# Two-chunk weight transfers over a longer part of the expert stream, and one early chunk in another buffer

## The chip, the core and the metric

The kernel runs on one core of a Trainium2 chip (trn2). The metric is device time in microseconds (us) of one launch: 1072.7 us, the median of three runs (1072.42 to 1074.67). One more execution was profiled. It took 1072.61 us, of which 1070.9 us are the span from its first to its last instruction.

In the rows, PE is TensorE's matmul side and PEld its weight load, DVE is VectorE, ACT is ScalarE, POOL is GpSimd and SP is SyncE, which here does little but wait on semaphores and issue DMAs.

## The reference

One encoder layer is computed for 320 tokens (256 of a prompt, 64 of a running stream) in float32, with D = 1024: a normalized input projection, sliding-window attention and a short convolution, an output projection, and then a mixture of 32 experts of which each token takes 4. The experts are what matters here:

```python
def expert_block(args):
    xe, e = args
    gu = xe @ w_gu[e] + b_gu[e]          # w_gu[e]: 1024 x 2048
    g, u = gu[:, :D_FF], gu[:, D_FF:]
    g = jnp.minimum(g, SWIGLU_LIMIT)
    u = jnp.clip(u, -SWIGLU_LIMIT, SWIGLU_LIMIT)
    h = (u + 1) * (g * jax.nn.sigmoid(SWIGLU_ALPHA * g))
    return h @ w_down[e] + b_down[e]     # w_down[e]: 1024 x 1024
```

All weights of all 32 experts are read from HBM once: 8 MB of `w_gu` and 4 MB of `w_down` for each, 418 MB read in all with the rest.

## The kernel before

**Work.** The attention part runs first (to about 155 us). Then the experts follow in 16 pairs. In a pair the two experts share the PE array: expert 2j fills rows 0 to 63 of the output and expert 2j+1 rows 64 to 127, so two matmuls of 64 rows go side by side. The weights of an expert are cut into 12 *chunks* of 1 MB (128 partitions x 2048 floats): chunks 0 to 7 are `w_gu`, used in `gate_up` (lines 891 to 903, matmuls on lines 896 and 898), and chunks 8 to 11 are `w_down`, used in `down` (lines 905 to 917, matmuls on lines 912 and 914). `pair(j)` computes gate and up of pair j, and then down of pair j-1; between them PE turns activations and one-hot matrices and scatters the rows of an earlier pair. Each use of a chunk adds one to the semaphore `chunk_used`; the chunks with the same number of the two experts of a pair come free practically together. `IN_USE` lists all 384 chunks in the order of their use.

**Loads.** A ring of 16 slots in SBUF receives the chunks in the order of `ORDER`, in which five chunks are left out: they have buffers of their own (`EARLY_AT`, `HALVES_AT`, `GU_AT`, `PIECES_AT`, `LATE_AT`) and are loaded once, by SP, before the ring comes round. 379 chunks go through the ring; here they are numbered 0 to 378 in load order. Chunk n goes to slot (n+1) mod 16. SP issues all loads from one queue, in order. A load of chunk n waits until chunk n-16, which had the slot before, has been used, that is until `chunk_used` has reached that chunk's place in `IN_USE` (line 495). Where SP waits, every later load waits behind it.

**One or two chunks to a transfer.** Lines 361 to 367 plan the transfers. Two chunks can go in one DMA if they are neighbours in HBM (an even chunk and the next one of the same expert) and lie in neighbouring slots. In `ORDER` such two stand next to each other, whereas `IN_USE` alternates between the experts; so the stretch with single transfers at the beginning (`EARLY` entries) and at the end (`FINE` entries) is copied from `IN_USE`. A two-chunk load waits for the later of its two slots, and both chunks count as landed when all of it has. Before the change chunks 0 to 36 go singly, two-chunk transfers run from chunk 37 to chunk 343 (with three single ones in between, where the alignment breaks at the left-out chunks), and chunks 344 to 376 go singly again. The last two chunks go in halves (line 502).

**PE and the loads.** PE waits for the landing of both chunks before each step of `gate_up` or `down` (`landed`, lines 886 to 889). `EARLY_AT` is chunk 11 of expert 1, a `w_down` chunk.

Of the kernel before, what the change touches and what calls it, by code (L numbers as in the profile page):

```python
# [29 lines left out]
def hybrid_layer_kernel(nc, x_prompt, x_sample, cache_k, cache_v, state_conv, norm1_g, w_in, q_norm_g,  # L30
# [14 lines left out]
    NE = w_router.shape[2]  # L45
# [16 lines left out]
    GUC, DNC = KT, FT * D // FLAT  # L62
    CH = GUC + DNC
# [7 lines left out]
    with ctx:  # L71
# [270 lines left out]
                    ORDER += [(2 * pair + s, c + a) for c in chunks[::2] for s in range(2) for a in range(2)]  # L342
        ALL = len(IN_USE)

        EARLY, FINE = 2 * 2 * GUC + 2 * DNC, 4 * GUC + 4
        ORDER[:EARLY] = IN_USE[:EARLY]
        ORDER[ALL - FINE:] = IN_USE[ALL - FINE:]
        EARLY_AT, LATE_AT, PIECES_AT = (1, CH - 1), (NE - 2, 0), (NE - 4, 0)
        HALVES_AT, GU_AT = (1, 3), (1, GUC - 1)
        for at in (EARLY_AT, LATE_AT, PIECES_AT, HALVES_AT, GU_AT):  # L350
            ORDER.remove(at)
# [1459 lines left out]
```

How the kernel before makes its waits and increments, by code:

```python
        def most_rows(eng):  # L403
            eng.wait_ge(counts_ready, 2)
            return eng.value_load(most_i[0:1, 0:1], min_val=0, max_val=TOK)
# [25 lines left out]
        @block.sync  # L431
# [23 lines left out]
                             ).then_inc(wo_in, 16)  # L455
            sp.dma_start(w_o[:, 0:CT, :],
                         w_out[0, ATT:ATT + CONV, :].rearrange("(j p) n -> p j n", p=P)).then_inc(wo_in, 16)
            load(*ORDER[RING - 1], 1, slot_of(RING - 1))
            FIRST_DONE = RING - 2
            for n in range(RING - 2):
                slot = slot_of(n)
                if slot == FREE_SLOTS:
                    sp.wait_ge(v_done, 1)
                if slot == QKV_SLOTS:
                    for q in range(2 * FF // (4 * P)):
                        sp.dma_start(b_guT[:, :, 4 * q:4 * q + 4],
                                     b_gu[0].rearrange("e (q p a) -> q p e a", p=P, a=4)[q]).then_inc(bias_in, 16)
                    sp.wait_ge(bch_done, 3 * CT)
                if slot == BCH_SLOTS:
                    sp.wait_ge(att_mixed, NCH)
                    sp.wait_ge(conv_mixed, CT)
# [3 lines left out]
                                     rows_of(*HALVES_AT, 1)[:, n2 * D:(n2 + 1) * D]).then_inc(halves_in, 16)  # L478
                if BCH_SLOTS <= slot < BCH_SLOTS + MIX // 2 - 1:
                    sp.wait_ge(wo_used, slot - BCH_SLOTS + 1)
                if slot == BCH_SLOTS + MIX // 2 - 1:
                    sp.wait_ge(out_done, 2 * NT)
                load(*ORDER[n], 1, slot)
```

## Time and profile before

| | |
|---|---|
| median of 3 runs | 1072.7 us |
| profiled execution | 1072.61 us |
| its span | 1070.9 us |
| PE busy | 1029.8 us, 96% |
| DVE, ACT, POOL busy | 30%, 9%, 1% |
| read from HBM | 418.29 MB, 392 GB/s over the span |
| the queue of the loads (q1) | 94.7% of 16 engines' span |

The span is read in stretches: an attention part, a stretch in which the experts' work goes on without a stop, one in which PE now and then waits for a load, and an end without such waits. Busy time by stretch, the chain of waits and the DMA queue's own waits are the views used.

### The profile page before, as it was taken

Reading aid. Unit: us, or ns where it says so; the run is one execution under the profiler, and the core shown is the slowest. Engines: PE = TensorE matmul, PEld = TensorE weight load, DVE = VectorE, ACT = ScalarE, POOL = GpSimd, SP = SyncE. Lnnn points to the kernel's source line nnn. Section 1 sums busy time; section 2 is a strip of 40 time slices with the busy share of each in tenths; the row PEclk is TensorE's granted clock in tenths of the full one; section 3 lists DMA queues with packets and bytes.
Section 4 is the critical chain, followed back from the end, with each engine's and each line's share of the span. In section 5 each row is a group of like instructions: output and inputs, shape, how many; then the busy total and the mean of one; then the engine's idle time right before and its main releaser. Section 6 shows DMA issues by size and latency. Waiting matters only on the chain.

```text
span 1070.9 us, 11705 instructions
## 1 busy us (share of the span) xinstructions
PE 1029.8 (96%) x5098; PEld 491.2 (46%) x5099; DVE 317.6 (30%) x491; ACT 95.9 (9%) x165; POOL 8.3 (1%) x20
## 2 busy tenths in 40 slices
PE   8999999999999999989898989989898989999998
PEld 7767454444444444435343534434353435334333
DVE  3533031323323232312313231323223232313243
ACT  2222040100000000000001010000000000100001
POOL 1100000000000000000000000000000000000000
PEclk9999999999999999999999999999999999999999
DMA  9950969999999999999999999999999999999996
GB/s 353 317 117 1 376 232 405 419 423 424 425 420 430 427 428 428 431 427 427 430 430 427 427 430 430 427 428 428 429 428 430 427 429 429 428 415 420 422 421 256
DMA packets 57470, 420.30 MB, mean 392 GB/s; under 512 B 21061, under 2 KB 21377, under 8 KB 28257
## 3 DMA queue, kind: packets, MB, share of 16 engines
q1 hardware_dynamic: 56848, 419.32, 94.7%
q0 software_dynamic: 352, 0.55, 0.2%
q8 instruction: 20, 0.33, 0.1%
q10 hardware_dynamic: 240, 0.03, 0.0%
q14 instruction: 10, 0.07, 0.0%
HBM read 418.29 MB, written 1.58 MB: 392 GB/s over the span
## 4 chain that ended last, share of the span: by engine, by line
PE 71%; DMA 28%; SPq 0%; issue 0%; DVE 0%; ACT 0%; DVEq 0%
PE ps L896 35%; DMA ring<-in_w_gu_dram 27%; PE ps L912 7%; PE ps L820 7%; PE ps L741 5%; PE ps L938 3%; PE ps L759 3%; PE ps L617 2%; PE ps L923 1%; PE ps L898 1%; PE ps L770 1%; PE ps L942 1%; PE ps L1074 1%; PE ps L643 1%; PE ps L709 0%; DMA x<-in_x_prompt_dram 0%
## 5 line engine op out<-in xcount | busy, mean ns | idle before, releaser
L896 PE MATMUL ps<-ring,xT 128*64 128x512 f32 x1008 | 457.2, 607 | 29.0 <-DMA ring<-in_w_gu_dram 28.7
L898 PE MATMUL ps<-ring,xT 128*64 128x512 f32 x1008 | 457.7, 608 | 0.0
L896 PEld LDWEIGHTS ps<-ring,xT 128*64 128x64 f32 x1008 | 135.8, 139 | 304.4 <-issue 300.1
L912 PE MATMUL ps<-ring,he 128*64 128x512 f32 x480 | 214.2, 595 | 3.9 <-DMA ring<-in_w_down_dram 3.0
L914 PE MATMUL ps<-ring,he 128*64 128x512 f32 x472 | 211.0, 596 | 0.0
L1667 DVE TENSOR_TENSOR x<-ps,x 128x512 f32<-128x512 f32 (+1 forms) x84 | 54.3, 684 | 295.7 <-PE ps L938 268.0
L898 PEld LDWEIGHTS ps<-ring,xT 128*64 128x64 f32 x1008 | 135.9, 139 | 0.0
L912 PEld LDWEIGHTS ps<-ring,he 128*64 128x64 f32 x480 | 62.8, 137 | 133.5 <-issue 133.2
L820 PEld LDWEIGHTS ps<-oh,hn 128*128 128x128 f32 x720 | 89.5, 196 | 8.2 <-issue 6.0
L820 PE MATMUL ps<-oh,hn 128*128 128x128 f32 x720 | 91.4, 282 | 0.0
L1309 ACT COPY gu_sb<-ps 128x1024 f32<-128x1024 f32 x16 | 16.2, 1012 | 596.0 <-PE ps L898 596.0
L914 PEld LDWEIGHTS ps<-ring,he 128*64 128x64 f32 x472 | 61.8, 137 | 0.0
L1618 DVE TENSOR_TENSOR xT<-ps,g 128x512 f32<-128x512 f32 (+2 forms) x35 | 22.5, 646 | 95.9 <-PE ps L820 95.9
L1650 DVE TENSOR_TENSOR xT<-ge,xT 128x1024 f32<-128x1024 f32 x16 | 19.6, 1224 | 91.0 <-PE ps L914 91.0
L1626 DVE COPY gu_sb<-ps 128x1024 f32<-128x1024 f32 x16 | 19.6, 1224 | 90.4 <-PE ps L898 90.4
L923 PEld LDWEIGHTS ps<-ident,gu_sb 128*128 128x128 f32 x256 | 32.1, 210 | 13.0 <-issue 13.0
L938 PE MATMUL ps<-y_hi,ohT 128*128 128x512 f32 x84 | 37.8, 450 | 0.0
L1634 DVE TENSOR_TENSOR ge<-ps,b_guT 128x1024 f32<-128x1024 f32 x16 | 19.6, 1225 | 58.6 <-PE ps L923 58.6
L741 PE MATMUL ps<-xnT,w_chc 128*128 128x320 f32 x128 | 36.5, 438 | 0.0
L923 PE MATMUL ps<-ident,gu_sb 128*128 128x128 f32 x256 | 35.1, 290 | 0.0
L938 PE MATMUL ps<-y_lo,ohT 128*128 128x512 f32 x84 | 33.2, 395 | 0.0
L938 PEld LDWEIGHTS ps<-y_hi,ohT 128*128 128x128 f32 x84 | 15.7, 187 | 38.0 <-issue 36.3
(233 smaller groups left out, 633.0 us busy)
## 6 DMA issues: line engine op xcount, KB each, us to landing
ring<-in_w_gu_dram SPq DMA_DIRECT2D x102, 2048.0 KB, 25.8
ring<-in_w_down_dram SPq DMA_DIRECT2D x50, 2048.0 KB, 27.0
ring<-in_w_gu_dram SPq DMA_DIRECT2D x48, 1024.0 KB, 15.5
ring<-in_w_down_dram SPq DMA_DIRECT2D x25, 1024.0 KB, 25.3
w_chc<-in_w_in_dram SPq DMA_DIRECT2D x1, 4096.0 KB, 21.1
w_qkv<-in_w_in_dram SPq DMA_DIRECT2D x4, 768.0 KB, 9.0
w_b<-in_w_in_dram SPq DMA_DIRECT2D x1, 2048.0 KB, 28.9
w_o<-in_w_out_dram SPq DMA_DIRECT2D x2, 1024.0 KB, 28.1
```

The source lines that it names most:

```text
L617: last = mm(ps[:, QK_BANK[i], t0:t1], w_qkv[:, k, cols], xnT[:, k, t0:t1], start=(k == 0 and t0 == 0), stop=(k == KT - 1), skip_group_chec ...
L741: last = mm(ps[:, BCH_BANK[part], 0:TOK], w[:, k, col:col + P], xnT[:, k, :], start=(k == 0), stop=(k == KT - 1))
L759: last = mm(ps[0:n, OUT_BANK[t][half], :], mixed(j, t, n), w_o[:, j, half * HALF:(half + 1) * HALF], start=(j == 0), stop=(j == MIX - 1))
L820: last = mm(out[:, k % (KT // 2), 0:experts * CAP], hn[:, t, tile_features(k)], marks[:, t, 0:experts, :].rearrange("p s c -> p (s c)"), s ...
L896: even = mm(gu_banks(j)[0:CAP, n, :], xT[j % 2][:, k, 0:CAP], first[n], start=(k == 0), stop=(k == KT - 1))
L898: odd = mm(gu_banks(j)[CAP:P, n, :], xT[j % 2][:, k, CAP:P], second[n], start=(k == 0), stop=(k == KT - 1))
L912: even = mm(out[0:CAP, half, :], hid[:, f, 0:CAP], first[2 * a + half], start=(f == 0), stop=(f == FT - 1))
L914: odd = mm(out[CAP:P, half, :], hid[:, f, CAP:P], second[2 * a + half], start=(f == 0), stop=(f == FT - 1))
L923: last = nc.tensor.transpose(by_feature(banks)[:, part, f, :], gu_sb[:, features(part, f)], ident[:, :])
L938: last = mm(ps[:, half, :], ohT[:, t * P:(t + 1) * P], y[:, cols], start=(y is y_hi), stop=(y is y_lo and u not in BIASED.get(j, ())), ski ...
L1618: return V.tensor_tensor(xT[j % 2][:, tiles, :], gathered_banks(j, half)[:, first:first + n, :], g2[:, tiles].unsqueeze(2).to_broadcast([P ...
L1667: V.tensor_tensor(x[0:m, t, cols], ps[0:m, bank, :], x[0:m, t, cols], ALU.add).then_inc(added, 1)
```

## The change

Three numbers of the plan change.

```diff
-        EARLY, FINE = 2 * 2 * GUC + 2 * DNC, 4 * GUC + 4
+        EARLY, FINE = 2 * GUC + 4, 4 * DNC
         ORDER[:EARLY] = IN_USE[:EARLY]
         ORDER[ALL - FINE:] = IN_USE[ALL - FINE:]
-        EARLY_AT, LATE_AT, PIECES_AT = (1, CH - 1), (NE - 2, 0), (NE - 4, 0)
+        EARLY_AT, LATE_AT, PIECES_AT = (1, 5), (NE - 2, 0), (NE - 4, 0)
```

With GUC = 8 and DNC = 4, `EARLY` goes from 40 to 20 and `FINE` from 36 to 16. Two-chunk transfers now start at chunk 17 and end with chunk 362; 20 chunks at the beginning (17 to 36) and 18 near the end (of 344 to 362) change from single to two-chunk transfers, and the plan has 19 transfers fewer. `EARLY_AT` is now chunk 5 of expert 1, a `w_gu` chunk that pair 0 uses, so chunk 11 of expert 1 goes through the ring. Chunks 10 to 35 of the ring are thereby others than before; the number of chunks in the ring and the bytes loaded stay the same.

What a load waits for, as the count of uses in `chunk_used`, worked out from the code:

| chunks | before | after |
|---|---|---|
| 16 | 1 | 1 |
| 17, 18 | 2; 3 | 3 |
| 19, 20 | 4; 5 | 5 |
| 21, 22 | 6; 7 | 7 |
| 23, 24 | 9; 10 | 10 |
| 25, 26 | 11; 12 | 13 |
| 27, 28 | 13; 14 | 15 |
| 29, 30 | 15; 17 | 18 |
| 31, 32 | 18; 19 | 20 |
| 33, 34 | 20; 21 | 23 |
| 35, 36 | 22; 23 | 24 |
| 37 with 38 | 25 | 27 |
| 39 with 40 | 27 | 28 |
| 49 with 50 | 37 | 39 |
| 51 with 52 | 39 | 40 |
| 53 with 54 | 43 | 43 |

From chunk 53 to chunk 343 both plans are the same.

SP's instructions where the ring first comes round, before and now (`const_room` is the last piece of a left-out chunk; 128x2048 is one chunk, 128x4096 are two; - is before, + is now):

```order
 L493 DMA gatesT_room<-in_w_gu_dram 128x512
 L493 DMA const_room<-in_w_gu_dram 128x512
-L438 DMA ring<-in_w_gu_dram 128x2048 x14
-L438 DMA ring<-in_w_down_dram 128x2048 x7
+L438 DMA ring<-in_w_gu_dram 128x2048
+L438 DMA ring<-in_w_gu_dram 128x4096 x6
+L438 DMA ring<-in_w_down_dram 128x4096 x4
 L438 DMA ring<-in_w_gu_dram 128x4096 x8
 L438 DMA ring<-in_w_down_dram 128x4096 x4
```

Where 21 single loads stood, one single load and ten of two chunks stand.

SP's instructions near the end, from pair 14's loads to the last chunks:

```order
 L438 DMA ring<-in_w_gu_dram 128x4096 x2
-L438 DMA ring<-in_w_down_dram 128x4096 x2
-L438 DMA ring<-in_w_down_dram 128x2048 x4
-L438 DMA ring<-in_w_gu_dram 128x2048 x15
+L438 DMA ring<-in_w_down_dram 128x4096 x4
+L438 DMA ring<-in_w_gu_dram 128x2048
+L438 DMA ring<-in_w_gu_dram 128x4096 x7
 L438 DMA ring<-in_w_down_dram 128x2048 x14
 L502 DMA ring<-in_w_down_dram 128x2x512 x4
```

18 of 19 single loads have become nine of two chunks; the last 14 and the halves stay. On PE the number and order of matmuls are the same; only four of pair 0 now read `early_chunk`, and four of the first `down` read the ring:

```order
-L898 MATMUL ps<-ring,xT_58 64x512
-L896 MATMUL ps<-ring,xT_58 64x512
-L898 MATMUL ps<-ring,xT_58 64x512
+L898 MATMUL ps<-early_chunk,xT_58 64x512
+L896 MATMUL ps<-ring,xT_58 64x512
+L898 MATMUL ps<-early_chunk,xT_58 64x512
```

## Rows read from the trace of the kernel before

**Rows 1.** Stretches: length; busy PE, PEld, DVE, ACT, POOL; clock, DMA share, GB/s

```profile
200.00:390.00 190.00, 190.00 (x981) 86.04 (x981) 58.04 (x74) 11.30 (x11) 0.00 (x0) 1.00 1.01 425
390.00:943.00 553.00, 520.07 (x2561) 234.35 (x2559) 157.05 (x202) 31.59 (x31) 0.52 (x1) 0.98 1.01 428
943.00:977.00 34.00, 34.00 (x154) 15.34 (x156) 5.16 (x8) 0.00 (x0) 0.00 (x0) 0.95 1.00 422
977.00:1054.00 77.00, 77.00 (x359) 28.82 (x355) 28.00 (x35) 6.36 (x6) 0.00 (x0) 1.00 1.01 420
```

**Rows 2.** PE's waits from 388 to 950 us: us in total, times, longest

```profile
PE ps L896 <- DMA ring<-in_w_gu_dram: 29.0, 14, 2.7
PE ps L912 <- DMA ring<-in_w_down_dram: 3.0, 9, 0.4
```

**Rows 3.** Chain of waits, 936 to 950 us: start us, us, what

```profile
914.51 28.28 DMA ring<-in_w_gu_dram
...
942.92 0.61 PE ps L896
```

**Rows 4.** SP's waits from 186 to 213 us

```profile
SPq L438 <- PE ps L898: 25.5, 6, 5.8
```

**Rows 5.** SP's issues, narrow windows from 107.9 to 246 us: start us, us, what

```profile
107.97 0.34 SPq L438 DMA_DIRECT2D ring<-in_w_gu_dram  x1
161.29 0.33 SPq L438 DMA_DIRECT2D ring<-in_w_gu_dram  x1
190.14 0.33 SPq L438 DMA_DIRECT2D ring<-in_w_gu_dram  x1
200.18 0.81 SPq L438 DMA_DIRECT2D ring<-in_w_down_dram  x2
209.33 0.33 SPq L438 DMA_DIRECT2D ring<-in_w_down_dram  x1
212.76 0.33 SPq L438 DMA_DIRECT2D ring<-in_w_gu_dram  x1
216.20 0.33 SPq L438 DMA_DIRECT2D ring<-in_w_gu_dram  x1
245.76 0.33 SPq L438 DMA_DIRECT2D ring<-in_w_gu_dram  x1
```

**Rows 6.** DMAs issued at 107.97, 161.29 and 212.76 us: count, KB, us to landing

```profile
ring<-in_w_gu_dram SPq DMA_DIRECT2D x1, 1024.0 KB, 5.2
...
ring<-in_w_gu_dram SPq DMA_DIRECT2D x1, 1024.0 KB, 6.7
...
ring<-in_w_gu_dram SPq DMA_DIRECT2D x1, 2048.0 KB, 9.8
```

**Rows 7.** The page: DMA issues of the whole span

```profile
ring<-in_w_gu_dram SPq DMA_DIRECT2D x102, 2048.0 KB, 25.8
```

**Rows 8.** PE in order of time from 942.5 us: start us, us, what [idle before]

```profile
942.92 0.61 PE L896 MATMUL ps<-ring,xT 128*64 128x512 f32 x1 [2.12 <-DMA ring<-in_w_gu_dram]
...
943.83 1.06 PE L896 MATMUL ps<-ring,xT 128*64 128x512 f32 x1
...
947.22 0.59 PE L896 MATMUL ps<-ring,xT 128*64 128x512 f32 x1
...
947.65 0.59 PE L896 MATMUL ps<-ring,xT 128*64 128x512 f32 x1
```

**Rows 9.** DMAs issued at 995.02 and 1041.97 us: count, KB, us to landing

```profile
ring<-in_w_gu_dram SPq DMA_DIRECT2D x1, 1024.0 KB, 24.2
...
ring<-in_w_down_dram SPq DMA_DIRECT2D x1, 512.0 KB, 17.8
```

**Rows 10.** PE in order of time, its first matmuls on what these two bring

```profile
1021.58 0.57 PE ps L896
...
1060.90 0.59 PE L1089 MATMUL ps<-ring,he_last 128*64 128x512 f32 x1
```

## The prediction

> **What bounds the kernel now.** I read the busy time by stretch first. From 200 us to 1054 us the DMA engines are busy without a gap (share 1.00 to 1.01), in stretches where PE is full (190 of 190 us to 390 us, then 34 of 34 and 77 of 77 us behind 943 us) and in one where it isn't (520 of 553 us) [rows 1]. So PE works faster than the loads come, lives on the stock in the ring until about 390 us, and is held by the loads from then on: 29.0 us in 14 waits and 3.0 us in nine [rows 2]. The last of these waits ends at 942.92 us, released by a load that landed at 914.51 + 28.28 = 942.79 us [rows 3]; behind it PE has no wait for a load and sets the end. The chain that decides the time is thus: the load queue up to 942.8 us, then PE. Everything that the load queue loses before 942.8 us and that no later pause gives back is lost at the end, since the queue has no pause in which to catch up. It may seem that early loads are not critical, as PE doesn't wait for them; but an idle microsecond of the queue at 210 us is one at 943 us as well.
>
> The second question is how full the queue is. A load spends 25.8 us from issue to landing in the median of two-chunk transfers [rows 7], some ten chunks' worth, but a load issued at 161.29 us only 6.7 us [rows 5, 6]. Around 200 us the queue is short because most of the ring still holds chunks that PE has not used, and SP waits for PE to free a slot: 25.5 us in six waits from 186 to 213 us, the longest 5.8 us [rows 4]. Here a later release can empty the queue.
>
> **The price of one chunk, and of a restart.** A chunk of 1024 KB is 1.0486 MB. At the 428 GB/s of the two-chunk stretch it takes 2.45 us, at the 420 GB/s of the single ones near the end 2.50 us [rows 1]. If the queue has run dry, the next load pays more than its bytes: the single chunk issued at 107.97 us, behind 36 us of SP waiting, landed 5.2 us later [rows 5, 6], which is 2.7 us above 2.50. I call that the restart. The nearest row that could give a larger one is the load at 161.29 us, 6.7 us to landing, so 4.2 us above its bytes; it stood behind three small pieces, so I take it as the upper bound. I take 2.7 us, since that row has, as the case in question, an empty queue ahead and further loads issued right behind. The lower bound is no restart at all, the bytes alone, as behind a full queue; with it the sum below is 2.7 us smaller.
>
> A page bears on this. The Trainium skill, DMA: Bandwidth & Descriptors, section Anatomy of one DMA — SWDGE (gpsimd) path, gives a DMA a fixed part of about 2.0 us beside its bytes, measured on another issuing path. These loads of SP show 2.7 us; with 2.0 the sum below would be 0.7 us smaller.
>
> **The change, walked through.** PE is full up to 390 us and waits for no load, so in the stretch to 260 us its uses, and with them the releases, come when they come now. They are read from the issues of before, where SP waited for them: use 15 at 190.14 us, use 19 and 20 at 200.18 us (two issues), use 23 at 209.33 us, use 25 at 212.76 us, use 27 at 216.20 us, use 39 at 245.76 us [rows 5]. Use 24 comes with 23.
> - Chunk 16 is issued at 161.29 us and lands at 161.3 + 6.7 = 168.0 us, as before [rows 5, 6].
> - Chunks 17 to 26 go as five pairs: 10 x 2.45 = 24.5, so to 192.5 us. Each is released before the queue has run dry.
> - Chunks 27, 28 now wait for use 15 (190.14 us): with the restart they can't start before 192.8, some 0.3 us idle. With 29, 30 the queue lasts to 192.8 + 4 x 2.45 = 202.6 us.
> - Chunks 31, 32 now wait for use 20 (200.2 us): start not before 202.9, landed at 207.8 us.
> - Chunks 33, 34 now wait for use 23, at 209.33 us; before, they were released one use-step earlier, in two single loads. PE takes 9.1 us from use 20 to use 23 and the queue had only two chunks, 4.9 us, to do. Start 209.33 + 2.7 = 212.0 us, 4.2 us after the queue ran dry; landed at 216.9 us. Chunks 35, 36 wait for use 24, so they are right behind: 221.8 us. Chunks 37, 38 wait for use 27 (216.20 us), before the queue is empty: 226.7 us.
> - Before, chunks 37, 38 landed at 212.76 + 9.8 = 222.6 us [rows 5, 6]. **The queue is 4.1 us late from here**, the smaller idle times before it and the saving of 20 chunks at 2.45 already in it. The value hangs on one release and one restart alone: 209.33 + 2.7 + 6 x 2.45.
> - Later pauses: the tightest of the following is chunk 49, which now waits for use 39 (245.76 us). The queue lasts to 226.7 + 10 x 2.45 = 251.2 us, and 245.8 + 2.7 = 248.5. It holds by 2.7 us. From chunk 53 to 343 both plans are alike, with no pause in the DMA engines before, and now the queue is 4.1 us fuller.
> - So PE meets its first wait earlier, waits 4 us longer in the sum, and its last wait ends at 942.92 + 4.1 = 947.0 us.
>
> **The end.** The 18 chunks that become pairs there save 18 x 0.05 = 0.9 us of the queue's time, all of it behind 943 us, where PE is full [rows 1]: worth nothing. Nor does it cost: SP issues these loads 24 us ahead of their landing [rows 9], so waiting one step of uses more (3.4 us, as from 212.76 to 216.20 us) [rows 5] leaves the queue filled. A pair counts as landed with its second chunk. The tightest case is chunk 6 of expert 31, which now comes with chunk 362: that landed at 995.02 + 24.2 = 1019.2 us and PE starts on chunk 6 at 1021.58 us [rows 9, 10], 2.4 us of room, and 0.9 more. The rehomed chunk costs nothing: in either plan its load stands in the queue ahead of chunk 16, which lands at 168.0 us, and PE can't begin step 6 of pair 0, which needs it, before 161.3 + 4 x 3.4 = 174.9 us, uses 1 and 2 having ended step 1 at 161.29 us; the matmuls are the same.
>
> Sum for the profiled execution: 1072.6 + 4.1 = 1076.7 us, span 1075.0; it stands 0.1 us under the median of the three runs, so the same number serves for it.
>
> **The rivals.**
> - *Restart of 4.2 us* instead of 2.7: all else alike, 5.6 us late, 1078.2 us. For it, the load of 161.29 us [rows 6]; against it, the three small pieces ahead of that one.
> - *The half-speed steps at 943 us go away.* After its last wait PE's matmuls took 1.06 instead of 0.59 us and started 0.85 apart instead of 0.43, for four steps from 943.83 to 947.22 us [rows 8], with a granted clock of 0.95 for the stretch [rows 1]: the lower clock level of 1.2 GHz after PE had stood idle 2.12 us. That costs 4 x 0.42 = 1.7 us, on the path. If in the shifted run it doesn't fall there, PE gains 1.7 us, and the loads allow it: the last one landed at 1041.97 + 17.8 = 1059.8 us, 1.1 us before its matmul [rows 9, 10], with 0.9 more from the pairs. 1075.0 us. Against it: the waits and the loads keep their pattern, only shifted.
> - *The queue doesn't run dry* (other side, no change or a little faster). The DMA engines would have to hold more work at 200 us than these landings show, or the restart be hidden by bytes still under way. Then only the rates count: 20 chunks x 0.05 = 1.0 us earlier at 943 us, with the end PE-bound: 1071.7 us. Decides if the gap between landing of chunk 32 and start of 33 is under 0.1 us. Against it: 9.1 us between the releases stand against 4.9 us of bytes. The Trainium skill, Perfetto Trace Analysis, section DMA Optimizations, speaks for this side: larger DMAs come nearer to the HBM's bandwidth. The trace agrees, by 2%, 428 against 420 GB/s [rows 1].
> - *The later landings make PE wait near the end*: if the pairs of 348 to 362 came over 3 us later than worked out, PE would wait once more; 1 to 2 us on top, 1078.5 us.
>
> **How the numbers follow.** Forecast 0.53, restart 0.17, clock 0.13, queue not dry 0.09, waits at the end 0.03, something else 0.05. The forecast's own spread (restart 2.0 to 3.4 us) is 1076.0 to 1077.4. The range goes from 1074.4 (the clock case with a restart of 2.1 us; the bound without any restart, 1074.0 us, lies just below) to 1078.5, leaving out the queue that is never dry and part of the rest. A difference under 0.2%, 2.1 us, can't be told from none. Slower by more than that: 0.84 (forecast, restart, end, clock nearly in full, as 2.4 us is just above). Same: 0.12. Faster: 0.04.
>
> **What would show it.** Right: a pause of the DMA engines of about 4 us near 208 to 212 us; the ring's two-chunk load released at about 209.3 us landing some 7.6 us later, and the next at 221.8; PE's waits for loads up by about 4 us from 32.0; the last of them ending at about 947 us; PE full behind it. Wrong: no pause near 210 us, or a pause that is there while the last wait of PE still ends at 943 us (then the queue has a reserve that I don't see), or new waits of PE on lines 896 and 912 behind 950 us.

## The result and the profile after

The changed kernel takes 1076.34 us (median of 10 runs, 1075.58 to 1077.0), the kernel before 1072.68 us (median of 10): 3.7 us slower, ratio 1.0030 with a 95% interval of 1.0022 to 1.0039. The forecast was 1076.7 us.

Busy time by stretch of the kernel after, columns as in [rows 1]:

```profile
200.00:390.00 190.00, 189.26 (x975) 86.04 (x977) 57.78 (x74) 11.03 (x11) 0.00 (x0) 1.00 0.99 419
390.00:943.00 553.00, 517.92 (x2557) 234.19 (x2555) 156.05 (x200) 31.86 (x31) 0.52 (x1) 0.98 1.01 428
943.00:981.00 38.00, 35.92 (x170) 16.35 (x170) 6.88 (x11) 0.43 (x1) 0.00 (x0) 1.00 1.01 421
981.00:1054.00 73.00, 71.80 (x335) 27.34 (x333) 26.27 (x33) 5.93 (x6) 0.00 (x0) 1.00 1.01 424
```

In the first stretch the DMA engines moved 419 GB/s instead of 425 [rows 1], which over 190 us are 1.1 MB or 2.7 us of the queue; from 390 to 943 us they move what they moved. A second loss lies ahead of these stretches, from 160 to 200 us, first before, then after:

```profile
160.00:200.00 40.00, 40.00 (x206) 17.03 (x202) 5.40 (x16) 2.29 (x2) 0.00 (x0) 1.00 1.00 408
```

```profile
160.00:200.00 40.00, 40.00 (x207) 17.16 (x204) 5.34 (x15) 2.29 (x2) 0.00 (x0) 1.00 0.98 391
```

(408 - 391) x 40 us = 0.68 MB or 1.6 us. Most of it is lost at the first pair: chunk 16 landed at 166.6 us here, 1.4 us sooner than in the first trace of before, and the pair behind it, released at 164.5 us, at 173.3 us, 6.8 us later for 4.9 us of bytes. The largest loss lies behind 200 us. The same view in steps of 2 us finds the place, in the kernel after:

```profile
207.00:209.00 2.00, 2.00 (x12) 0.64 (x10) 1.53 (x3) 0.00 (x0) 0.00 (x0) 1.00 0.29 123
209.00:211.00 2.00, 2.00 (x12) 0.65 (x10) 0.00 (x0) 0.00 (x0) 0.00 (x0) 1.00 0.64 123
211.00:213.00 2.00, 2.00 (x12) 0.72 (x10) 0.00 (x0) 0.00 (x0) 0.00 (x0) 1.00 0.85 319
```

and in the kernel before:

```profile
207.00:209.00 2.00, 2.00 (x12) 0.71 (x10) 1.74 (x3) 0.00 (x0) 0.00 (x0) 1.00 1.01 397
209.00:211.00 2.00, 2.00 (x12) 0.72 (x10) 0.00 (x0) 0.00 (x0) 0.00 (x0) 1.00 1.01 422
211.00:213.00 2.00, 2.00 (x12) 0.57 (x8) 0.00 (x0) 0.00 (x0) 0.00 (x0) 1.00 1.01 422
```

The last column is what counts: (397 + 422 + 422 - 123 - 123 - 319) x 2 us = 1.35 MB less, 3.2 us at 428 GB/s. PE is full in both, so PE's rows alone would not show it.

SP's issues in narrow windows of the kernel after, against [rows 5], and the landings of the loads of 189.94, 209.12 and 215.99 us, against [rows 6]:

```profile
189.94 0.33 SPq L438 DMA_DIRECT2D ring<-in_w_gu_dram  x1
...
209.12 0.33 SPq L438 DMA_DIRECT2D ring<-in_w_down_dram  x1
...
215.99 0.33 SPq L438 DMA_DIRECT2D ring<-in_w_gu_dram  x1
```

```profile
ring<-in_w_gu_dram SPq DMA_DIRECT2D x1, 2048.0 KB, 8.8
...
ring<-in_w_down_dram SPq DMA_DIRECT2D x1, 2048.0 KB, 7.7
...
ring<-in_w_gu_dram SPq DMA_DIRECT2D x1, 2048.0 KB, 11.2
```

Chunks 33, 34 are issued at 209.12 us and land at 216.8 us (forecast 216.9); 37, 38 land at 227.2 us (forecast 226.7) instead of 222.6.

PE's waits for loads, the first two rows from 388 to 955 us, against [rows 2], the third behind 956 us, where there was none:

```profile
PE ps L896 <- DMA ring<-in_w_gu_dram: 33.2, 16, 2.7
PE ps L912 <- DMA ring<-in_w_down_dram: 3.3, 10, 0.4
...
PE ps L912 <- DMA ring<-in_w_down_dram: 1.2, 1, 1.2
```

32.0 us have become 36.5. The chain of waits, against [rows 3], and PE in order of time, against [rows 8]:

```profile
918.16 28.18 DMA ring<-in_w_gu_dram
946.33 0.14 issue
946.47 0.61 PE ps L896
```

```profile
946.47 0.61 PE L896 MATMUL ps<-ring,xT 128*64 128x512 f32 x1 [2.08 <-DMA ring<-in_w_gu_dram]
...
946.92 0.59 PE L896 MATMUL ps<-ring,xT 128*64 128x512 f32 x1
...
947.35 0.59 PE L896 MATMUL ps<-ring,xT 128*64 128x512 f32 x1
```

The same load releases PE 3.55 us later than before. But the matmuls behind it run at 0.59 us each, a step every 0.43 us: the four steps of 0.85 us [rows 8] are missing. The granted clock says the same, from 940 to 960 us, first before, then after:

```profile
940.00:960.00 20.00, 17.88 (x78) 8.32 (x78) 3.36 (x5) 0.00 (x0) 0.00 (x0) 0.91 1.00 411
```

```profile
940.00:960.00 20.00, 17.92 (x86) 8.33 (x84) 2.67 (x4) 0.18 (x1) 0.02 (x1) 1.00 1.01 413
```

### The profile page after: what moved, and what is told of

Its sections match the earlier page's. It is cut to its first block, busy times and chain, and to the rows that moved or that the text cites. A ratio compares the mean times of both kernels' runs of the same rounds, so it can differ in the third digit from the quotient of the medians.

```text
span 1074.2 us, 11686 instructions
## 1 busy us (share of the span) xinstructions
PE 1027.5 (96%) x5098; PEld 492.0 (46%) x5099; DVE 317.6 (30%) x491; ACT 96.0 (9%) x165; POOL 8.3 (1%) x20
## 4 chain that ended last, share of the span: by engine, by line
PE 66%; DMA 33%; SPq 0%; issue 0%; DVE 0%; ACT 0%; DVEq 0%
PE ps L896 34%; DMA ring<-in_w_gu_dram 30%; PE ps L820 8%; PE ps L741 5%; PE ps L912 5%; PE ps L938 3%; PE ps L759 3%; DMA ring<-in_w_down_dram 2%; PE ps L617 2%; PE ps L898 1%; PE ps L923 1%; PE ps L770 1%; PE ps L942 1%; PE ps L1074 1%; PE ps L643 1%; PE ps L709 0%
## 5 line engine op out<-in xcount | busy, mean ns | idle before, releaser
L896 PE MATMUL ps<-ring,xT 128*64 128x512 f32 x1008 | 453.6, 604 | 33.5 <-DMA ring<-in_w_gu_dram 33.3
L898 PE MATMUL ps<-ring,xT 128*64 128x512 f32 x1000 | 450.8, 604 | 0.0
L741 PE MATMUL ps<-xnT,w_chc 128*128 128x320 f32 x128 | 36.5, 438 | 0.0
```

The source lines that it names most:

```text
L741: last = mm(ps[:, BCH_BANK[part], 0:TOK], w[:, k, col:col + P], xnT[:, k, :], start=(k == 0), stop=(k == KT - 1))
L896: even = mm(gu_banks(j)[0:CAP, n, :], xT[j % 2][:, k, 0:CAP], first[n], start=(k == 0), stop=(k == KT - 1))
L898: odd = mm(gu_banks(j)[CAP:P, n, :], xT[j % 2][:, k, CAP:P], second[n], start=(k == 0), stop=(k == KT - 1))
```

## The experiments

Theory Q: the change empties the load queue near 209 us, and what the queue loses there shows at the end. Rival P: the cost lies in the two-chunk transfers themselves, by their number. Rival E: it lies near the end. Each kernel was timed in 5 rounds beside the kernel before (1072.9 to 1073.3 us in these series), unless said otherwise.

**Holding one load, with no pair added.** The kernel before, one wait lengthened:

```diff
-                sp.wait_ge(chunk_used, max(used_up_to(*ORDER[n - RING]) for n in range(first, first + many)))
+                sp.wait_ge(chunk_used, max([{33: 23}.get(first, 0)] + [used_up_to(*ORDER[n - RING]) for n in range(first, first + many)]))
```

> The kernel before, all its single and two-chunk transfers unchanged; only the load of chunk 33 waits for use 23 (209.3 us) instead of use 20 (200.2 us). Theory Q (an empty load queue near 209 us is what the change costs): start at 209.3 + 2.7 = 212.0 us, four single chunks at 2.5 us, chunk 36 lands at 222 us instead of 217.5, so +4.4 us on the time, less or more by the 1 us steps in which landings jitter; 1076 to 1077 us. Rival P (the two-chunk transfers themselves cost, as a pair lands only with its second chunk): no pair is added, so no change, 1072.7 us. Rival E (the end of the stream costs): no change either.

Measured: 1077.35 us against 1072.92, ratio 1.0041 (1.0028 to 1.0055), 4.4 us slower. All of the change's cost with none of its transfers; that it is 0.7 us more than the change's 3.7 is within the two intervals. The gap in this kernel:

```profile
207.00:209.00 2.00, 2.00 (x12) 0.66 (x10) 1.97 (x3) 0.00 (x0) 0.00 (x0) 1.00 0.00 0
209.00:211.00 2.00, 2.00 (x12) 0.72 (x10) 0.15 (x1) 0.00 (x0) 0.00 (x0) 1.00 0.21 41
211.00:213.00 2.00, 2.00 (x12) 0.62 (x10) 0.00 (x0) 0.00 (x0) 0.00 (x0) 1.00 0.87 291
```

By the last column (397 + 422 + 422 - 0 - 41 - 291) x 2 = 1.82 MB less than before, 4.2 us.

**One step more**, `{33: 25}` in the same place.

> As the run before, but chunk 33 waits for use 25, one step of 3.4 us later (212.8 us). Theory Q: slope one, so 3.4 us more than with use 23, +7.8 us over the kernel before, 1080.5 us. Theories P and E: no change. If PE or a reserve in the ring absorbed part of an early gap, the step would be under 3.4 us.

Measured: 1080.46 us, ratio 1.0071 (1.0057 to 1.0085), 7.5 us slower and 3.1 us more than with use 23. The load of chunk 33 was issued at 212.77 us instead of 209.71, so 3.1 us later (3.4 were expected). This step of the queue's idle time at 210 us comes out at the end one for one. Neither PE nor the ring's stock takes anything of it up; PE only has a wait for a load before 380 us now, 1.9 us long, and is held by the loads from there on as before.

**The same hold where the queue is full**, `{205: 199}`.

> The kernel before with a longer hold, 11 us instead of 9, but on the load of chunk 205, which now waits for use 199 (620.9 us) instead of use 195 (609.9 us), where the queue holds some ten chunks. Theory Q: the queue has work until 630.9 us, the hold ends 10 us before, so no gap and no change, 1072.7 us. A theory in which each late issue costs by itself, wherever it is, gives +5 to +11 us.

Measured: 1073.18 us, ratio 1.0003 (0.9994 to 1.0012): not told from nothing, and far from 5 to 11 us. The waits of SP from 605 to 625 us, and the stretches from 610 to 630 us, in this kernel:

```profile
SPq L438 <- PE ps L898: 21.2, 1, 21.2
```

```profile
610.00:620.00 10.00, 10.00 (x58) 5.49 (x56) 3.00 (x5) 0.00 (x0) 0.00 (x0) 1.00 1.01 431
620.00:630.00 10.00, 9.66 (x53) 4.62 (x51) 4.10 (x4) 1.94 (x2) 0.00 (x0) 1.00 1.00 426
```

SP waits 21 us in one piece, where in the kernel before it was two waits of at most 10.2 us, and the DMA engines move 431 and 426 GB/s all the same: the load issued at 621.92 us instead of 609.92 has others ahead of it until 631.9 us. Here the late issue leaves nothing idle and costs nothing. Against the first trace of before, chunk 200 landed 1.0 us later in this one and chunk 220 just as much, so the hold between them added nothing.

**The end of the change alone**, `FINE = 4 * DNC` in the kernel before.

> Only the end part of the change: two-chunk transfers up to chunk 362, the beginning and the early buffer as before. Theory Q with PE bound at the end: the queue finishes 0.9 us earlier, the time is the same, 1072.7 us (down to 1071 if PE's half-speed steps near 943 us don't fall on the path in most executions). Rival E: the pairs' later landings make PE wait, 1 to 4 us slower.

Measured: 1073.09 us, ratio 1.0000 (0.9991 to 1.0009). Rival E falls; nor is a gain to be seen (the interval leaves room for 1 us either way).

**The beginning of the change alone**, `FINE = 4 * GUC + 4` in the changed kernel.

> The beginning of the change (two-chunk transfers from chunk 17, chunk 5 of expert 1 in the early buffer) with the end as before. Theory Q: the whole cost stands here, 1076.3 to 1077.3 us; up to 0.8 us more than the full change if, in the shifted run, the loads and not PE bound the end, since 18 chunks there take 0.05 us more each. Rival E (the end carries the cost): 1072.7 us.

Measured: 1076.76 us, ratio 1.0032 (1.0020 to 1.0044). The whole cost is there. The 0.4 us above the full change is of the sign expected, but within the noise.

**The beginning taken apart.** First the other early chunk alone, `EARLY_AT = (1, 5)` in the kernel before:

> Only the other chunk in the early buffer; all transfers as before. The chunks of the ring from 10 to 35 are one place further on in the order of use, so the loads of 26 to 38 wait for one use more. Theory Q, walked through: chunks 31, 32 wait for use 19, 20 (200.2 us) and start at 202.9 instead of 202.6, chunk 33 waits for use 21 (205.9 us) and starts at 208.6, 0.8 us after the queue ran dry; chunk 36 lands at 218.6, +1.1 us, 1073.8 us. Rival (the rehoming costs nothing, as predicted): 1072.7 us.

Measured: 1073.44 us, ratio 1.0007 (0.9998 to 1.0016), 0.4 us slower, not told from nothing; the interval, to 1.7 us, holds the expected 1.1 us too. Then the early pairs without it, `EARLY = 2 * GUC + 4` in the kernel before:

> Two-chunk transfers from chunk 18, but chunk 11 of expert 1 in the early buffer and the end as before. Theory Q: chunks 32, 33 wait for use 20 (200.2 us) with chunk 31 ahead of them, so the queue lasts to 210.0 us; 34, 35 wait for use 23 (209.3 us), start at 212.0, 2.0 us idle; chunk 36 lands at 219.4 instead of 217.5, +1.9 us, 1074.6 us. Rival P (the number of early pairs sets the cost): as the full change, 1076.3 us, since nine of ten early pairs are there.

Measured: 1074.73 us, ratio 1.0016 (1.0007 to 1.0025), 1.7 us slower (expected 1.9). Rival P's 3.6 us lie outside the interval. So the rehoming is a part of the cost after all: with the early pairs it moves chunk 33 from the release by use 20 to that by use 23, and 1.7 us become 3.7. Alone, neither makes the full gap.

**One pair of the changed kernel taken apart**, `and n != 33` in the condition for two chunks:

> The changed kernel with one pair taken apart: chunks 33 and 34 go singly, so 33 waits for use 21 (205.9 us) and 34 for use 23 (209.3 us). Theory Q: 33 starts at 208.6 us (0.8 us idle) and lands at 211.1; 34 starts at 212.0 (0.9 us idle) and lands at 214.5; 35, 36 at 219.4 us instead of 221.8, so 2.4 us less than the full change, 1073.9 to 1074.3 us. Rival P: one pair of 20 undone, 0.2 us less, 1076.1 us.

Measured: 1075.60 us against 1073.01, ratio 1.0019 (1.0010 to 1.0028). 2.6 us slower than before, so about 1.1 us less than the full change, where the walk gave 2.4 and rival P 0.2. The direction is Q's, the size isn't, and with intervals of 0.9 us on either side the time alone doesn't tell 1.1 us from rival P's 0.2. The trace shows why it is so little: chunk 32, which by the walk lands at 207.8 us, landed at 210.5 us here. The queue was 1.2 us behind the walk at chunk 26 already (193.7 instead of 192.5 us), and the releases at 190.1 and 200.2 us cost 1.0 us each, where the walk had 0.3. The split could only win what was left, and chunk 38 landed at 226.4 instead of 227.2 us.

**Pairs, but not at the tight place**: `EARLY = 2 * GUC + 4, FINE = 4 * DNC` in the kernel before, and one line that puts chunks 30 to 36 back in the order of use:

```diff
+        ORDER[4 * GUC:4 * GUC + 2 * DNC] = IN_USE[4 * GUC:4 * GUC + 2 * DNC]
```

> Six two-chunk transfers at the beginning (chunks 18 to 29) and the nine near the end, chunk 11 of expert 1 in the early buffer; chunks 30 to 36 single in the order of use, so that at the tight place 31, 32, 33 and 34 are released by use 18, 19, 20 and 21 as in the kernel before. Theory Q: no gap, 12 chunks at 0.05 us less, 0 to 0.6 us faster than before, 1072.1 to 1072.7 us. Rival P (cost by the number of pairs): six of ten early pairs, about 2 us slower, 1075 us.

Measured: 1073.73 us against 1073.26, ratio 1.0006 (0.9997 to 1.0015). Six early pairs and nine near the end cost less than 1.6 us, where rival P wants 2. The hoped for 0.6 us didn't come. It is no version that beats the kernel before. Nor did the early part leave the queue untouched: chunks 31 to 34 are released as before, but chunk 35 waits for use 23 (209.3 us) instead of use 22, since the chunk that had its slot came in pair order. The DMA engines moved 328 GB/s from 211 to 213 us against 422 in the kernel before, and chunk 38 landed at 224.7 us instead of 222.6.

**A hold that should barely touch the queue's end**, `{31: 19}` in the kernel before.

> The kernel before, with the load of chunk 31 waiting for use 19 (200.2 us) instead of use 18 (193.9 us). By a queue with one server, as in the prediction's walk: chunk 30 lands at 202.6 us, 31 can start at 202.9, 0.3 us idle, then 32 and 33 at once, so +0.3 us, 1073.0 us. If the 16 DMA engines run dry one after the other before the last of them lands a chunk, the loss is larger than the gap between landings: +1 to +3 us, as two kernels before this one showed their chunk 31 late.

Measured: 1073.12 us against 1073.26, ratio 1.0001 (0.9992 to 1.0010). The first expectation (0.3 us) is within the interval, the second's 1 to 3 us are not, but for its lower end. The engines did run short, as the second had it, 1 us steps from 200 us:

```profile
200.00:201.00 1.00, 1.00 (x8) 0.76 (x7) 0.00 (x0) 0.00 (x0) 0.00 (x0) 1.00 0.34 139
201.00:202.00 1.00, 1.00 (x10) 1.00 (x10) 0.41 (x1) 0.00 (x0) 0.00 (x0) 1.00 1.02 188
202.00:203.00 1.00, 1.00 (x8) 0.59 (x9) 0.97 (x2) 0.00 (x0) 0.00 (x0) 1.00 0.66 229
```

which is 0.7 MB or 1.7 us under the full rate, although chunk 31 was issued while earlier ones were still to land. Chunk 38 landed 1.8 us later than in the kernel before, and PE's last wait ended 0.1 us later. So a short drain is paid for at once and can be given back later.

**Second traces of both kernels**, one execution each (1073.84 and 1076.97 us).

> The kernel before once more, for a second trace: the steps of about 1.1 us that its landings show at chunks 56 and 84. If they belong to the plan they come at the same chunks; if they come from other traffic on the 16 engines they move, and the queue's lag at 390 us moves by 1 us with them.

> The changed kernel once more, for a second trace: the gap at 208 to 210 us and the landing of chunk 34 at 216.8 us must come again, within 0.3 us; the steps of 1.1 us may move.

Before: the steps come again at the same two chunks, 56 and 84. But they don't belong to the plan: in two other kernels that have the same plan there (the end alone, and the hold of chunk 205) one stands at chunk 66 (landed at 292.4 and 294.2 us) and none at chunk 84. In the first trace of before the load of 252.62 us landed after 9.1 us, the one issued right behind it, at 253.38 us, after 14.3:

```profile
ring<-in_w_down_dram SPq DMA_DIRECT2D x1, 2048.0 KB, 9.1
...
ring<-in_w_down_dram SPq DMA_DIRECT2D x1, 2048.0 KB, 14.3
```

that is at 261.7 and 267.7 us, 6.0 us for 4.9 us of bytes. In the changed kernel the same two, issued at 252.42 and 252.79 us:

```profile
ring<-in_w_down_dram SPq DMA_DIRECT2D x1, 2048.0 KB, 14.9
...
ring<-in_w_down_dram SPq DMA_DIRECT2D x1, 2048.0 KB, 19.4
```

267.3 and 272.2 us, 4.9 us. From the landing of chunk 36 to that of chunk 114 the kernel before takes 193.1 and 194.3 us in its two traces, the changed one 191.9 and 191.3, the two that held chunk 33 191.1 and 191.3; the bytes alone are 78 x 2.45 = 191.1. After: the gap is there again, the pair issued at 209.76 us landed 7.5 us later, at 217.3 instead of 216.8, in a run that is shifted by half a us from the start. Its landing was expected within 0.3 us and missed that.

**All traces side by side**, one execution each, in us from the start of the span:

| kernel | chunk 38 lands | PE's last wait for `w_gu` ends | span |
|---|---|---|---|
| end alone | 222.6 | 942.3 | 1070.3 |
| before | 222.6 | 942.9 | 1070.9 |
| before, second | 222.4 | 943.9 | 1071.9 |
| chunk 205 held | 222.3 | 944.0 | 1071.8 |
| chunk 31 held | 224.3 | 943.1 | 1071.0 |
| pairs 18 to 29 | 224.7 | 944.2 | 1071.1 |
| rehomed only | 225.2 | 943.3 | 1071.8 |
| early pairs only | 225.5 | 944.7 | 1073.0 |
| pair 33 split | 226.4 | 945.5 | 1073.5 |
| changed | 227.2 | 946.5 | 1074.2 |
| beginning alone | 227.9 | 947.0 | 1074.8 |
| changed, second | 228.0 | 947.0 | 1075.2 |
| chunk 33 to use 23 | 228.4 | 947.0 | 1075.4 |
| chunk 33 to use 25 | 231.3 | 950.2 | 1078.5 |

From PE's last wait to the end it is 127.7 to 128.5 us in thirteen of the fourteen, whatever was done to the queue, and 126.9 us in the one with the pairs 18 to 29. So the span follows the last wait, as theory Q has it: it moves with it from 942.3 and 1070.3 to 950.2 and 1078.5 us. The way from chunk 38 to the last wait isn't as even: the ten traces that are late at chunk 38, by 1.8 to 8.8 us against the first trace of before, are 0.9 to 2.2 us less late at the last wait. The DMA engines show where, from 250 to 300 us, first before, then after:

```profile
250.00:300.00 50.00, 50.00 (x259) 22.54 (x255) 13.55 (x19) 2.98 (x3) 0.00 (x0) 1.00 1.00 420
```

```profile
250.00:300.00 50.00, 50.00 (x259) 22.62 (x257) 13.75 (x19) 3.18 (x3) 0.00 (x0) 1.00 1.01 428
```

All ten late ones moved 427 or 428 GB/s there, the four others 417 to 421.

## Why the prediction was right

**Where the bound lies**: right. Loads up to the last wait of PE, PE behind it. The waits of PE rose by 4.5 us (forecast 4), the last ended at 946.47 us (forecast 947.0).

**The gap**: right in place and cause. One release, by use 23 at 209.1 us, decides. Taking away every other part of the change and keeping this release gives 4.4 us; taking it away and keeping most of the pairs gives 0.5 us, not told from nothing. What the queue loses ahead of 209 us (1.6 us before 200 us, more behind it) doesn't add to the sum: it makes the gap at 209 us shorter, since the release ends the gap in any case: 1.35 MB are missing from 207 to 213 us in the changed kernel, 1.82 MB where the hold stands alone.

**The restart of 2.7 us**: right for this pair (7.7 us to landing, 4.9 of bytes, so 2.8; 2.6 in the second trace), but not a constant, and in part luck. Behind an empty queue too, chunk 33 paid 5.1 - 2.5 = 2.6 us when held to use 23, and 6.2 - 2.5 = 3.7 us when held to use 25. The trace of before itself had a second such load, which the prediction doesn't weigh: issued at 146.85 us behind 18.7 us of SP waiting, 6.1 us to landing, so 3.6 us above its bytes. With that one the forecast would have been 1077.6 us. The pair of 189.94 us paid less than its 8.8 - 4.9 = 3.9 us seem to say, as the load ahead of it landed only at 192.9 us: 5.8 us from landing to landing, so 0.9 us lost.

**The losses before the gap**: undersized. The walk treats the queue as one server that loses nothing as long as a load is issued 2.7 us before the last one lands. Yet from landing to landing the first pair, issued 2.0 us before chunk 16 landed, lost 1.9 us, and the pairs released at 189.9 and 200.0 us, with 3.0 and 3.9 us of work ahead, lost 0.9 and 0.3 us. The walk had 0, 0.3 and 0.3. The landings of the walk came near all the same (192.5 forecast and 192.9 measured for chunk 26) because it took chunk 16 for 168.0 us, as in the first trace of before, and that chunk landed 1.4 us sooner in this run: luck. None of this did harm to the sum, which hangs on the last release alone; it made the expectation for the split of chunk 33 wrong by 1.3 us.

**"The queue is 4.1 us late from here" to the end**: the queue was 4.6 us late at chunk 38 (227.2 against 222.6), 5.6 us at chunk 44 after a step of its own, and 3.5 us at PE's last wait. The walk assumed that a lag stays to the microsecond. Some 2 us were given back between 250 and 340 us, in two steps that the kernel before takes and the changed one doesn't. The errors of opposite sign, 0.5 us too small at chunk 38 and 1.1 us too large behind it, left 0.6 us too much. In the second traces the last wait ends at 943.89 us before and at 947.04 after, 3.2 us apart, and the two traces of before differ by 1.0 us. That the forecast came within 0.4 us of the median is thus in part luck.

**The rehomed chunk at no cost**: wrong as a sentence by itself, though not in the sum. Its buffer and its matmuls cost nothing, but it moves the ring's later chunks by one place, and without that the early pairs cost 1.7 us instead of 3.7. The walk had the counts of uses with the rehoming in them, which is why the sum didn't suffer.

**The end, PE-bound throughout**: wrong in its detail, and the prediction's own sign for it came, a new wait of PE on line 912 behind 950 us. In the profiled run the rival in which the half-speed steps go away is what happened, and PE gained 1.7 us. But that rival took it that the loads allow it, looking at the last load only, and there it failed. The tighter place is the first `w_down` chunk of expert 31: before, it landed at 1044.07 us and PE began on it at 1045.40, so 1.3 us of room. Now it landed 4.4 us later, with another step of 0.7 us in the landings at 1031 us taking most of what the nine pairs saved, while PE was 3.55 - 1.7 = 1.85 us later: 4.4 - 1.85 - 1.3 = 1.2 us of waiting, as measured at 1048.6 us. The 1.7 us were thus worth 0.3: from the last wait to the end it is 127.7 us instead of 128.0.

The steps aren't tied to the change. They follow PE's last wait in seven of the fourteen traces, among them the hold of chunk 33 to use 23 and the split, and are missing in seven, among them the kernel before with chunk 31 held, whose queue is on time again there. In that trace, too, PE gained the steps and then waited for the same chunk:

```profile
PE ps L912 <- DMA ring<-in_w_down_dram: 1.3, 1, 1.3
```

So the end costs the same either way, and the forecast of 4.1 us holds with a PE that is held by the loads at one more place. The second trace of the changed kernel has no such wait and its half-speed steps later, near 1008 us. Only the trace with the pairs 18 to 29 and those near the end has neither the steps nor the wait, and it has the shortest end, 126.9 us; that is one execution, and the kernel's median isn't lower.

**The rule on larger transfers**: bigger ones move 428 GB/s against 420 [rows 1], and where that was the main thing that changed (the end alone, the pairs 18 to 29) no gain in time could be told.

## What to carry to other kernels

In a kernel that the load queue bounds later on, look for the place where the queue is shortest, not for the place where the engine waits: the time from issue to landing tells it, 6.7 us there against 26 us in the rest. A transfer of two slots waits for the later of both; where the queue holds under three chunks and releases come in bursts, such a delay empties it, while a longer one is free where it holds ten. Change the order of a ring and check every release at the tight place again, also for a change that seems to move one buffer only.

## What was not expected of the hardware

The queue of loads is 16 engines, and they don't run dry together. With chunk 31 held to 200.3 us, the engines moved 139 and 188 GB/s from 200 to 202 us, with a DMA share of 0.34 in the first of the two, although the chunk ahead landed only at 202.3 us.

A queue that has once run short flows more evenly afterwards. From the landing of chunk 36 to that of chunk 114 the four traces without a shortage took 192.8 to 194.6 us, the ten with one 190.8 to 191.9, where the bytes are 191.1. That is how part of a loss comes back: what is missing are steps in the landings that the others take, mostly of about 1 us, one of 2.3. One reading is that the engines drift apart, by small traffic of their own such as instruction loads, and that a gap levels them. The instruction queue's share, 263 to 268 us, before and after:

```profile
q8 instruction: 1, 0.02, 1.3%
```

```profile
q8 instruction: 1, 0.02, 1.4%
```

One such load falls there in both kernels, and only the one before shows a step; so such a load alone doesn't make it, and which engine it hits isn't seen in these records. The cause stays open.

The clock's fall after PE's last wait isn't told by how long PE stood idle. After idle times of 1.96 to 2.22 us it fell to 1.2 GHz in seven traces (a granted clock of 0.91 over 20 us), after 2.08 to 2.42 us it did not in the other seven (1.00). Nor is such a wait needed: in the second trace of the changed kernel it fell at about 1007.6 us, with PE busy without a gap:

```profile
1000.00:1005.00 5.00, 5.00 (x23) 1.57 (x20) 1.24 (x2) 0.00 (x0) 0.00 (x0) 1.00 1.03 439
1005.00:1010.00 5.00, 5.00 (x12) 1.53 (x14) 1.38 (x2) 0.00 (x0) 0.00 (x0) 0.76 1.00 426
```

What decides it stays open.
